# A 64-row, 64-column product in front of the column-block streams of a two-model float32 forward pass

## The reference

```
x = x + concat(gating(p), rwkv7(p)) @ ev_w_out      # p = rmsnorm(x) @ ev_w_in
x = x + ffn0(rmsnorm(x))                            # w_up 1024 x 5632, w_down 2816 x 1024
x = x + dilated_attention(rmsnorm(x) @ od_w_qkv) @ od_w_out
x = x + ffn1(rmsnorm(x));  x = rmsnorm(x)
# second model: every norm is followed by a scale and a shift made from silu(c) @ w_ada
x = x + g * (moba_attention(h @ w_qkv_2) @ w_o_2);   x = x + g * swiglu(h)     # ffn2
x = x + g * (short_conv(h @ w_in_2) @ w_out_2);      x = x + g * swiglu(h)     # ffn3
```

## Time and profile before

| | |
|---|---|
| median of 3 runs | 1339.16 us (1337.71 to 1341.57) |
| profiled execution, its own time | 1343.52 us |
| its span | 1341.7 us |
| PE matmul busy | 1288.0 us (96%) |
| VectorE (DVE) busy | 949.3 us (71%) |
| ScalarE (ACT) busy | 691.2 us (52%) |
| DMA moved | 263.77 MB, mean 197 GB/s |

### The profile page before, as it was taken

How to read it: one execution, slowest core, us unless ns; L and a number is a source line. 1 busy time by engine, 2 the same in 40 slices (tenths; PEclk the granted TensorE clock), 3 DMA queues, 4 the chain that set the end, 5 groups by cost and what they waited for, 6 DMA issues and landing times.

```text
span 1341.7 us, 24056 instructions
## 1 busy us (share of the span) xinstructions
PE 1288.0 (96%) x10267; PEld 1192.6 (89%) x10267; DVE 949.3 (71%) x1242; ACT 691.2 (52%) x987; POOL 16.5 (1%) x26
## 2 busy tenths in 40 slices
PE   6988999999999999999999997999999999999998
PEld 5978879999989978999998995899999899899997
DVE  5774348888867565888886577689997676676453
ACT  5932448655564544855557544644343644644441
POOL 0002000000000000000000000000000000000000
PEclk9988899999999989999999999999999999999999
DMA  9450226877458404677744542599996355675551
GB/s 308 150 189 2 66 82 233 270 250 240 153 202 300 173 17 126 236 266 251 251 157 142 189 144 78 191 316 353 361 354 243 118 197 189 209 270 179 182 191 38
DMA packets 161572, 263.77 MB, mean 197 GB/s; under 512 B 3565, under 2 KB 95929, under 8 KB 161466
## 3 DMA queue, kind: packets, MB, share of 16 engines
q1 hardware_dynamic: 160586, 259.54, 56.7%
q10 hardware_dynamic: 880, 2.69, 0.6%
HBM read 261.17 MB, written 1.05 MB: 195 GB/s over the span
## 4 chain that ended last, share of the span: by engine, by line
PE 87%; DVE 7%; ACT 4%; issue 1%; DMA 1%; DVEq 0%; ACTq 0%
PE ps L1014 23%; PE ps L985 15%; PE ps L986 15%; PE ps L987 15%; PE ps L2174 2%; PE ps L771 2%; DVE wlo L562 2%; PE ps L773 2%; PE ps L772 2%; PE ps L751 1%; PE ps L2467 1%; DVE arena L1987 1%; ACT whi L556 1%; DMA ring<-in_ev_w_in_dram 1%; PE ps L1000 1%
## 5 line engine op out<-in xcount | busy, mean ns | idle before, releaser
L562 DVE TENSOR_TENSOR wlo<-ring,whi 128x2048 fp32r<-128x2048 f32 x195 | 445.3, 2287 | 133.1 <-ACT whi L556 133.1
L985 PE MATMUL ps<-ghi,whi 128*128 128x256 f32 x1632 | 460.3, 282 | 0.0
L986 PE MATMUL ps<-glo,whi 128*128 128x256 f32 x1632 | 455.8, 279 | 0.0
L987 PE MATMUL ps<-ghi,wlo 128*128 128x256 f32 x1632 | 455.2, 279 | 0.0
L556 ACT ACTIVATE whi<-ring 128x2048 fp32r<-128x2048 f32 x195 | 372.2, 1913 | 136.4 <-PE ps L1014 118.8
L985 PEld LDWEIGHTS ps<-ghi,whi 128*128 128x128 f32 x1632 | 306.6, 188 | 2.1 <-issue 1.7
L986 PEld LDWEIGHTS ps<-glo,whi 128*128 128x128 f32 x1632 | 306.0, 188 | 2.1 <-issue 1.7
L987 PEld LDWEIGHTS ps<-ghi,wlo 128*128 128x128 f32 x1632 | 306.0, 188 | 0.0
L1014 PE MATMUL ps<-whi,yhi 128*128 128x512 f32 x480 | 160.6, 399 | 1.2 <-DVE ylo L1787 0.8
L1014 PE MATMUL ps<-wlo,yhi 128*128 128x512 f32 x480 | 157.2, 393 | 0.0
L1014 PE MATMUL ps<-whi,ylo 128*128 128x512 f32 x480 | 156.3, 391 | 0.0
(11 more groups left out here) (294 smaller groups left out, 1602.7 us busy)
## 6 DMA issues: line engine op xcount, KB each, us to landing
arena<-in_w_ada_dram SPq DMA_DIRECT2D x48, 1024.0 KB, 6.5
ring<-in_ff_w_up_dram SPq DMA_DIRECT2D x44, 1024.0 KB, 7.6
ring<-in_w_gate_up_dram SPq DMA_DIRECT2D x44, 1024.0 KB, 7.1
ring<-in_ff_w_down_dram SPq DMA_DIRECT2D x10, 2048.0 KB, 7.9
ring<-in_w_down_dram SPq DMA_DIRECT2D x10, 2048.0 KB, 7.9
ring<-in_od_w_qkv_dram SPq DMA_DIRECT2D x6, 2048.0 KB, 8.1
ring<-in_w_qkv_dram SPq DMA_DIRECT2D x6, 2048.0 KB, 7.8
ring<-in_w_in_dram SPq DMA_DIRECT2D x6, 2048.0 KB, 8.0
```

Source lines behind the costliest of these rows:

```text
L562: e.tensor_tensor(shaped(WLO[i % NB], k), v, shaped(WHI[i % NB], k).bitcast(F32), ALU.subtract).then_inc(S["w_lo"], 1)
L985: e.matmul(o, wh, h[0][:, k, :], start=k == 0, stop=False)
L986: e.matmul(o, wh, h[1][:, k, :], start=False, stop=False)
L987: x = e.matmul(o, wl, h[0][:, k, :], start=False, stop=k == NK - 1)
```

## The change

`pe_tile` gets a flag `small`. Where it is set, one product stands in front of the tile's 48: 64 rows, 64 stationary columns of the weights' high part and 64 moved columns of the activations' high part, both in fp32r, written to the corner of the tile's own bank. The tile's first product overwrites it (its `start` is True), so it leaves no trace in the result. The flag is set for a tile that follows a row block, a row sum, turns or adaptive sums in the ffns, the first qkv stage and cin; it isn't used in the second model's qkv stage. There are 40 such products: 9 each in ffn0, ffn1 and ffn2, 8 in ffn3, 3 in qkv and 2 in cin. Nothing else changes.

```diff
-        def pe_tile(e, w, key, k_norm, fresh, pair=False, turned=()):
+        def pe_tile(e, w, key, k_norm, fresh, pair=False, turned=(), small=False):
...
             h = ht(k_norm)
+            if small:
+                e.matmul(ps[0:64, 0:64], hi[0:64, 0:64], h[0][0:64, 0, 0:64], start=True, stop=True)
             for a in range(2):
...
-                pe_tile(e, w, ("qkv", m // 2, m % 2), 2, False, False, [("qkv", 0, q) for q in range(2)] if m == 2 else ())
+                pe_tile(e, w, ("qkv", m // 2, m % 2), 2, False, False, [("qkv", 0, q) for q in range(2)] if m == 2 else (),
+                        m in (2, 3) or ADA["qkv"]["sums", ("tile", m)])
...
-                        [("cin", 1, 0, q) for q in range(2)] if m == 2 else ())
+                        [("cin", 1, 0, q) for q in range(2)] if m == 2 else (), m in (2, 3))
...
         def pe_ffn(e, w, f, k_norm):
             pe_first(e, w, k_norm)
-            kept = []
+            kept, small = [], True
             for what, i in walk(f):
+                small = small or what == "rows" or what == "sums" and bool(i)
                 if what == "tile" and i >= 2:
-                    pe_tile(e, w, ("up", f, i), k_norm, False, True, [("up", f, j) for j in range(2)] if i == 2 else ())
+                    pe_tile(e, w, ("up", f, i), k_norm, False, True, [("up", f, j) for j in range(2)] if i == 2 else (),
+                            small)
+                    small = i == 2
```

## The result

| | before | after |
|---|---|---|
| median of 7 runs, taken together | 1341.57 us (1337.71 to 1344.20) | 1350.88 us (1347.34 to 1354.03) |
| ratio, 95% interval | | 1.0069 [1.0050, 1.0087] |
| profiled execution, its own time | 1343.52 us | 1350.88 us |
| its span | 1341.7 us | 1349.1 us |

The change costs 9.3 us at the medians, 0.7%. The forecast was 1336.0 with a range up to 1345.5.

What follows compares the result with a forecast made beforehand. The prediction took PE, busy 96%, as the bound: 15.4 us lost minus 18.6 gained is −3.2 on the profiled 1343.52, so 1340.3; carrying over that execution's 4.4 us above the median gave 1336.0 us, range 1333.0 to 1345.5.

Steps and rivals of the forecast that it cites:

- What bounds the kernel: PE is the bound, busy 96% of the span; inside tile stages only the spacing of products counts.
- The two rates: Tile streams run at 117.8 or 113.4 ns a product, kept from the first few products to the end.
- 264 products counted as already fast: Two tile pairs in ffn2 (192) and tile 2's first half in ffn0, ffn2 and ffn3 (72), excluded from the gain.
- Where is the fast rate dependable? The row blocks show it: Row blocks, sized like tile products, hold 43 products in 4.6 us behind a 64-row product, 41 otherwise.
- five of five: All five row blocks directly behind 64-row products, one at 38 us and four in the attention, run fast.
- the term of 18.6 us: Gain in tile streams if all 40 land fast: 4200 products at 4.42 ns each.
- 41 where none did: Row blocks without a 64-row product in front were said to hold 41 products in 4.6 us, not 43.
- The price: Each small product on PE costs 0.385 us, bounds 0.325 to 0.505, for changing form twice; 15.4 us lost.
- The 0.375 for one pass fewer: Small product's price if fp32r saves one f32 pass from 0.405 us; 0.385 was taken, a third of the way up.
- The stream stays slow: Rival: tile streams stay at 117.8 ns, leaving +15.4 and +1.2 for the 264 once fast: 1355.8 us; chance 0.10.
- Some land fast, some don't: Rival: only part of the tile streams turn fast; three in four gives 1340.7, half 1345.3; chance 0.15.
- Nearly free: Rival: small products cost only 0.03 us each, 1.2 us lost and 17.4 gained: 1321.8; chance 0.04.

Runs made afterwards that it cites:

- e11: Kernel before plus one full-row fp32r product of 16 columns in front of twelve tiles directly behind row sums in ffn0, ffn1 and ffn3; 1335.14 us, ratio 0.9956.
- e8: The kernel before run once more, no edit; 1341.11 us.
- e4: Kernel before with the change's 64x64 product in front of each half of every row block and nowhere else; 1342.67 us (before 1342.47).
- e1: Changed kernel with its 40 small products made f32, 64 rows, 128 stationary and 256 moved columns; 1366.37 us (before 1342.47).
- e2: Changed kernel with another 64-row product form by stage, fp32r or f32, 64 or 128 stationary, 64 to 256 moved columns; 1358.05 us (before 1342.47).
- e3: Changed kernel with the small product given 128 rows and 128 stationary columns, 64 moved, fp32r; 1344.27 us (before 1342.47).
- e5: Changed kernel with full-row products of 16 to 256 moved columns at the 40 places, f32 in ffn2 and ffn3, otherwise fp32r; 1344.10 us (before 1339.96).
- e9: Changed kernel with a short full-row product instead behind row sums and at three ffn2 places, elsewhere a 512-column and a short one; 1345.98 us (before 1343.95).
- e10: The changed kernel run a third time, no edit; 1356.93 us (before 1343.95).
- e12: e11 plus an fp32r product of 64 rows, 128 stationary, 256 moved columns in front of tile 3 of six stages; 1335.59 us, ratio 0.9962.
- e7: The changed kernel run again, no edit; 1349.80 us (before 1339.96).

## Why the prediction was wrong

**What bounds the kernel** was read rightly. PE is still the bound, 96% busy; a gap on PE is paid in full, stage by stage, and a faster spacing is gained nearly in full (3.5 of 3.8 us in the three stages of e11).

**The two rates** were read rightly as well, and so was their lasting to the end of a stream. They are the same, 113.3 and 117.8, in all fourteen traces. Of the 264 products counted as already fast, the 72 of tile 2 only carried on the rate of `pe_first`, which comes out otherwise in another execution (e8).

**The step that failed** is the sentence "Where is the fast rate dependable? The row blocks show it", and with it "five of five", which carried the term of 18.6 us and a chance of 0.66. Those five were few kinds of place: four are the same code repeated in the attention, all behind one f32 product of 64 rows, 128 stationary and 256 moved columns. I took the property that the five had in common and that the change also has, 64 rows, for the cause. The 18.6 us came out as a loss of 1.2. The runs show in its place that 64 rows in front don't set the rate; more of what stands ahead counts:
- the same product in front of the same stream gives fast and slow in turn (e4);
- in front of tiles 64 rows with 64 stationary columns give 0 of 89, with 128 stationary columns some of each (e1, e2);
- 128 rows do it too, behind row sums with 16, 32, 128 or 160 columns and not with 64 or 96 (e3, e5);
- the fifth of the five ran slow in e1, e9 and e11, with nothing changed ahead of it.

"41 where none did" was misread too: the earlier trace rows shows one such block. The trace before has another, in the second model's attention, with 128-row products (L2427, L2428) in front of it, and it is fast:

```profile
792.50:797.10 4.60, 4.60 (x43) 1.00 0.51 155
```

The prediction had more warnings in its hands and weighed them too lightly: the products of the trace were f32 and 128 columns wide and stood in front of row blocks; and behind adaptive sums (L2464) alone two tile streams had come out fast, with no 64-row product near. A rate that comes in fast without the supposed cause isn't set by it. The gain should have been given even odds at most, and the slow side most of the range.

**The price** held. Predicted 0.385 us each between 0.325 and 0.505, measured 0.369; 15.4 us against 14.8. By parts: between the small product's start and the tile's first 0.17, where 0.20 stood; between the tile's first and second 0.23, where 0.22 stood. The 0.375 for one pass fewer was nearer than the third of the way up.

**The rival "The stream stays slow"** is what happened, and it named both terms, 15.4 and 1.2. Its 1355.8 us is where e10 lies (1356.9, with the stretch at the lower clock in it). The median of 1350.9 is nearer to before by something that the prediction had no term for: 5.6 to 7.0 us in the first attention come and go with the granted clock. The 4.4 us between the profiled execution and the median of three runs were carried over as a constant; they are spread of the same kind (the profiled execution had a mean clock of 0.983, and later executions of before at 0.983 took 1343.5 and 1343.9 us, at 0.988 1337.7 and 1338.6).

**"Some land fast, some don't"** did not happen with the change (0 of 40), but some forms with 128 stationary columns gave it (11 of 40 in e1, 6 of 40 in e2). **"Nearly free"** is wrong even without the change of form: 0.11 us in e3, not 0.03.

The Trainium skill, "TensorE: Matmul & The Clock Gate", Back-to-back issue gap, has one formula for the gap, about 109 ns for 256 columns. The page gives it for products taken by themselves and says that in a stream of weight loads and products, as here, both set the spacing; the prediction left that out. By the formula no product in front could have gained anything, which would have given the right sign for this change. But the traces have two gaps, 113.3 and 117.8, and e11 gains by going from one to the other: the rule does not explain the loss, it only leaves out what was hoped for.

## What to carry to other kernels

A rate that shows in a few places of a trace is not a rule until the same sequence in front gives it in different places: count kinds of place, not occurrences, and look for places that have the rate without the supposed cause. On a kernel bound by TensorE, a product in another form of the array cost 0.35 to 0.82 us in a stream of fp32r products, by its size and type, and a short one in the stream's own form 0.11. A try at one place of each kind tells more than any argument: the full-row fp32r product of 16 or 32 columns behind 512-column sums was fast in 38 of 38 places over four kernels, and twelve of them alone came with 0.4%.

## What the runs showed of the hardware

- A stream of fp32r products, 128 stationary and 256 moved columns with a weight load each, has two stable spacings at the granted clock of 1.00: 113.3 and 117.8 ns. It settles within the first eight products and then holds, here for up to 432 products at the fast rate (49 us in cin of e12) and 456 at the slow (cin in before).
- In front of tiles, the length, form and type of the products ahead bear on which one it takes, and not monotonically: behind 512-column sums, full-row fp32r products of 16, 32, 128 and 160 columns give the fast one, of 64, 96, 192, 224 and 256 the slow one. Why there are two stays open.
- Some places come out differently in two executions of the same kernel, so the sequence ahead isn't all: of the 672 products of `pe_first`, 144 were fast in after, 216 in e7 and 288 in e10, a difference of up to 0.6 us.
- The granted clock falls to 1.2 GHz for 13.7 to 17.1 us in the first attention, where PE has pauses, in twelve of fourteen traces, and not in the other two. The windows with and without it differ by 5.6 to 7.0 us, beside the 9.3 that the change was measured to cost.
